# Latent attention scores as row halves plus one stacked rotated product, and bias tables masked one pair per weight piece

## What is computed

```python
def mla_dense(qn, qr, kn, kr, v):
    # qn (B,q,H,64), qr (B,q,H,32), kn (B,k,H,64), kr (B,k,32) shared by the heads, v (B,k,H,64); H = 8
    s = (einsum('bqhd,bkhd->bhqk', qn, kn) + einsum('bqhr,bkr->bhqk', qr, kr)) * (64 + 32) ** -0.5
    p = softmax(s, axis=-1)
    return einsum('bhqk,bkhd->bqhd', p, v)
```

## Time and profile before

| | |
|---|---|
| Runs shown | 2302.57, 2307.16, 2306.70 us; median 2306.7 |
| Profiled execution | 2304.6 us, of which span 2302.8 |
| Granted TensorE clock | 0.996 of full speed |
| PE busy | 2236.8 us, 97% of the span |
| DVE, ACT, POOL busy | 56%, 40%, 12% |
| Chain that ended last | PE 86%, DVE 5%, ACT 3%, ACT's queue 2% |
| DMA queue of ACT | 38914 packets, 33.69 MB |

### The profile page before, as it was taken

How to read it: one execution, slowest core, us unless ns; L and a number is a source line. 1 busy time by engine, 2 the same in 40 slices (tenths; PEclk the granted TensorE clock), 3 DMA queues, 4 the chain that set the end, 5 groups by cost and what they waited for, 6 DMA issues and landing times.

```text
span 2302.8 us, 32992 instructions
## 1 busy us (share of the span) xinstructions
PE 2236.8 (97%) x13479; PEld 1856.5 (81%) x13479; DVE 1294.3 (56%) x1884; ACT 926.4 (40%) x1558; POOL 277.3 (12%) x175
## 2 busy tenths in 40 slices
PE   7999999999999999999999999999989999999999
PEld 7876688888778776688888888888878888888887
DVE  4687558963224778459963225414666562225884
ACT  3447743222214447742222223223655333123773
POOL 2001222121332002221211000000000000000000
PEclk9999999999999999999999999999999999999999
DMA  5220025632983210035532321221000214212221
GB/s 159 87 69 2 1 95 179 198 114 76 235 219 97 83 56 1 7 133 173 165 123 78 128 93 56 78 83 42 15 15 15 81 56 160 84 55 74 68 66 55
DMA packets 149417, 205.80 MB, mean 89 GB/s; under 512 B 42485, under 2 KB 95746, under 8 KB 149250
## 3 DMA queue, kind: packets, MB, share of 16 engines
q1 hardware_dynamic: 110288, 169.83, 22.8%
q10 hardware_dynamic: 38914, 33.69, 5.5%
q0 software_dynamic: 64, 0.16, 0.0%
HBM read 188.85 MB, written 14.82 MB: 88 GB/s over the span
## 4 chain that ended last, share of the span: by engine, by line
PE 86%; DVE 5%; ACT 3%; ACTq 2%; issue 2%; POOL 1%; DMA 1%; POOLq 0%; DVEq 0%
PE ps L526 62%; PE ps L1858 4%; PE ps L1892 3%; PE ps L2509 3%; PE ps L1909 3%; ACTq L2248 2%; PE ps L2526 2%; PE ps L2538 2%; PE ps L2514 1%; PE ps L733 1%; DVE neg_max L2060 1%; DVE probs_t L2116 1%; ACT probs_t L2615 1%; ACT w_high L486 1%; DVE w_low L491 1%
## 5 line engine op out<-in xcount | busy, mean ns | idle before, releaser
L491 DVE TENSOR_TENSOR w_low<-w_raw,w_high 128x2048 fp32r<-128x2048 f32 (+4 forms) x140 | 308.6, 2205 | 497.0 <-ACT w_high L486 496.8
L486 ACT ACTIVATE w_high<-w_raw 128x2048 fp32r<-128x2048 f32 (+4 forms) x140 | 253.0, 1807 | 617.6 <-PE ps L526 559.3
L526 PE MATMUL ps<-h_hi,w_high 128*128 128x512 f32 (+1 forms) x1168 | 439.5, 376 | 1.6 <-DVE h_lo L2906 1.0
L526 PE MATMUL ps<-h_lo,w_high 128*128 128x512 f32 (+1 forms) x1168 | 437.1, 374 | 0.0
L526 PE MATMUL ps<-h_hi,w_low 128*128 128x512 f32 (+1 forms) x1168 | 436.8, 374 | 0.0
L526 PEld LDWEIGHTS ps<-h_hi,w_high 128*128 128x128 f32 x1168 | 220.0, 188 | 42.7 <-issue 1.4
L526 PEld LDWEIGHTS ps<-h_hi,w_low 128*128 128x128 f32 x1168 | 219.8, 188 | 39.7
L526 PEld LDWEIGHTS ps<-h_lo,w_high 128*128 128x128 f32 x1168 | 220.0, 188 | 38.9 <-issue 0.5
L526 PE MATMUL ps<-w_high,h_hi 128*128 128x512 f32 (+3 forms) x576 | 214.0, 372 | 0.7 <-DVE h_lo L2906 0.7
L526 PE MATMUL ps<-w_low,h_hi 128*128 128x512 f32 (+3 forms) x576 | 211.6, 367 | 0.0
L526 PE MATMUL ps<-w_high,h_lo 128*128 128x512 f32 (+3 forms) x576 | 211.3, 367 | 0.0
(11 more groups left out here) (372 smaller groups left out, 3880.5 us busy)
## 6 DMA issues: line engine op xcount, KB each, us to landing
w_raw<-in_w_gate_up SPq DMA_DIRECT2D x44, 1024.0 KB, 5.2
ada_w<-in_ada_w SPq DMA_DIRECT2D x24, 1024.0 KB, 5.2
w_raw<-in_w_down SPq DMA_DIRECT2D x20, 1024.0 KB, 5.1
w_raw<-in_w_in SPq DMA_DIRECT2D x16, 1024.0 KB, 5.1
w_raw<-in_c_in_w SPq DMA_DIRECT2D x16, 1024.0 KB, 5.4
w_raw<-in_w_out SPq DMA_DIRECT2D x8, 1024.0 KB, 5.0
w_raw<-in_ab_in_w SPq DMA_DIRECT2D x8, 1024.0 KB, 5.1
mask_table<-bias_scratch ACTq DMA_DIRECT2D x32, 224.0 KB, 7.8
```

Source lines behind the costliest of these rows:

```text
L486: e.activation(w_high[j % 2][:, 0:size], w_raw[j % 2][:, 0:size], ACT.Copy).then_inc(sig.w_high_done, 1)
L491: e.tensor_tensor(w_low[j % 2][:, 0:size], w_raw[j % 2][:, 0:size], w_high[j % 2][:, 0:size].bitcast(F32), ALU.subtract).then_inc(sig.w_lo ...
L526: mm = e.matmul(dst, lhs, rhs, start=start and a == 0, stop=stop and a == 2)
```

## The change

*Latent scores.* The plain rows of both heads of a pair go into one tile of 128 rows (head 0 in rows 0 to 63, head 1 in rows 64 to 127), and their three products run as row halves in `ORDER`, as in the window. The rotated rows of a head are stacked on 96 rows: the query's as high, high, low and the key's as high, low, high, so that one product on 96 rows gives all three terms. It is added last, except for head 1's context columns, where it comes just before the wait. The stacked keys are the same for all heads and are turned once (two turns at iterations 10 and 11). `rope3` holds three copies of the 32 rotated columns; GpSimd makes those of the next pair's queries after each second unit. The six turns of a pair stand at -4, -4, -3, -3, -2, -2. The queries of window pair 0 are turned before the keys. The queries' evacuation (`QueriesOut`) writes plain and rotated columns apart, two operations for one.

*Bias.* Each piece from 2 to 9 carries the loads of one pair, each from 4 to 11 the store of one.

```diff
-        kvx = at("kvx", [P, NA, BH, 160], F32, R2 + 18432)
+        kvx = at("kvx", [P, NA, 2, BH * 64], F32, R2 + 18432)
+        rope3 = at("rope3", [P, NA, 2, 96], F32, R2 + 18432 + 24576)
...
+        class QueriesOut(InvertedOut):
+            def put(self, e, d, src, mine, m):
+                inv = lat_inv[:, self.group, m:m + 1]
+                for n, (dst, part) in enumerate(zip(d, (src[:, :, 0:64], src[:, :, 64:96]))):
+                    dst = dst.rearrange("p (h w) -> p h w", h=4)
+                    ins = e.activation(dst, part, ACT.Copy, scale=inv) if mine == 0 else e.tensor_scalar(dst, part, inv, None, ALU.mult)
+                ins.then_inc(sig.evac_act if mine == 0 else sig.evac_vec, 1)
...
-                self.paired = [self.local(s) and units[self.steps[s][0]].kind != "mla" for s in range(N)]
+                self.paired = [self.local(s) > 0 for s in range(N)]
...
+                    def rope(dst, m, a, b, block):
+                        return e.matmul(dst.rearrange("p (b c) -> p b c", c=P), x.q_rope(m, block), x.k_rope(a, b), start=False, stop=True)
+
                     if not nl:
                         for c, j in enumerate(js):
                             for n in range(3):
                                 for m in range(2):
-                                    mm = third(self.row(s, m * len(js) + c), m, NT, NA, n, block=x.tiles[j][0])
-                    elif x.kind == "mla":
-                        for m in range(2):
-                            for n in range(3):
-                                third(here[m], m, lo, lo + nl, n)
-                                mm = third(there[m], m, NT, NA, n)
+                                    mm = third(self.row(s, m * len(js) + c), m, NT, NA, n, x.kind != "mla", block=x.tiles[j][0])
+                            for m in range(2 if x.kind == "mla" else 0):
+                                mm = rope(self.row(s, m * len(js) + c), m, NT, NA, x.tiles[j][0])
                     else:
                         for where, n in self.ORDER:
                             m = int(where[1])
+                            if where == "T0" and n == 0 and x.kind == "mla":
+                                rope(there[1], 1, NT, NA, block).then_inc(sig.half_scored, 1)
                             if where == "T0" and n == 0:
                                 e.wait_ge(sig.half_scored, B["half_scored"] + sum(map(bool, self.paired[:s + 1])))
...
+                        if x.kind == "mla":
+                            for m in range(2):
+                                rope(here[m], m, lo, lo + nl, block)
+                            mm = rope(there[0], 0, NT, NA, block)
                     mm.then_inc(sig.scores_ready, 1)
...
+                    if kind in ("parts", "ropes"):
+                        for m in range(2):
+                            ins = e.activation(dst[m], src[:, m * 2 * P:m * 2 * P + 2 * P].rearrange("p (b c) -> p b c", c=P), ACT.Copy)
...
-                    e.tensor_copy(kvx[:, :, :, 128:160], bc(k_rope.unsqueeze(2), [P, NA, BH, 32])).then_inc(sig.rope_staged, 1)
+                    e.tensor_copy(rope3[:, :, 0, :].rearrange("p t (c w) -> p t c w", c=3), bc(k_rope.unsqueeze(2), [P, NA, 3, 32])).then_inc(sig.rope_staged, 1)
...
+                    p = (u - 5) // 2
+                    if not self.grid and u % 2 and 0 <= p < BH // 2:
+                        e.wait_ge(sig.qk_bank, B["qk_bank"] + turned[p] + 1)
+                        for m in range(2):
+                            src = q_b[:, :, 512 + 64 * p + 32 * m:544 + 64 * p + 32 * m]
+                            e.tensor_copy(rope3[:, :, m, :].rearrange("p t (c w) -> p t c w", c=3), bc(src.unsqueeze(2), [P, NA, 3, 32])).then_inc(sig.rope_staged, 1)
...
-            LOADS, STORES = {2: (0, 1), 3: (2, 3), 6: (4, 5), 7: (6, 7)}, {4: (0, 1), 5: (2, 3), 8: (4, 5), 9: (6, 7)}
...
-                for n in self.LOADS.get(j, ()):
+                n = j - 2
+                if 0 <= n < self.PAIRS:
+                    if n >= 2:
+                        e.wait_ge(sig.bias_masked, B["bias_masked"] + n - 1)
                     if n >= 4:
-                        e.wait_ge(sig.bias_stored, B["bias_stored"] + 64)
+                        e.wait_ge(sig.bias_stored, B["bias_stored"] + 16 * (n - 2))
                     for m in range(2):
                         for half in range(2):
...
-                for n in self.STORES.get(j, ()):
+                n = j - 4
+                if 0 <= n < self.PAIRS:
                     e.wait_ge(sig.bias_masked, B["bias_masked"] + n + 1)
                     e.dma_start(masked_dram[n], mask_tables[n % 4][:]).then_inc(sig.bias_stored, 16)
...
-                at_ = [20 + 5 * p + c for c in (-6, -5, -4, -3, -3, -2)]
...
+                at_ = 20 + 5 * p
+                turns.append((at_ - 4, 4 + p, qn[:, 0:4, :], lambda x, f=q_nope: f(x), P, 4, None, ""))
...
+                for m, d in ((0, -4), (1, -3)):
+                    turns.append((at_ + d, 4 + p, stack(m)[:, 0:4, :], lambda x, m=m, f=q_rope: f(x, m), 96, 4, staged, "64"))
...
+                turns.append((at_ - 3, 4 + p, [stack(m)[:, 4:6, :] for m in range(2)], lambda x, f=q_rope: f(4 + x % 2, x // 2), 96, 4, staged, "ropes"))
...
+                turns.append((at_ - 2, 4 + p, kn[:, 0:4, :], lambda x, f=k_nope: f(x), P, 4, None, ""))
...
+                turns.append((at_ - 2, 4 + p, [qn[:, 4:6, :], kn[:, 4:6, :]], lambda x, f=q_nope, g=k_nope: f(4 + x) if x < 2 else g(2 + x), P, 4, None, "parts"))
```

More of the change, by code:

```diff
@@ L1703, in build_program, with __init__ @@
         class WideUnit:
-            def __init__(self, kind, group, head, chunk, t0, tiles, q, k, value, q_low=None, k_low=None):
+            def __init__(self, kind, group, head, chunk, t0, tiles, q, k, value, q_low=None, k_low=None, q_rope=None, k_rope=None):
+                self.q_rope, self.k_rope = q_rope, k_rope
                 self.q_low, self.k_low = q_low, k_low
@@ L1768, in __init__ @@
                 else:
[L1769 removed]
+                    self.counts.update({"keys_staged": 2, "rope_staged": 1 + BH})
             def unit(self, s):
@@ L1875, in scores @@
                             if where[0] == "H":
-                                mm = third(here[m], m, lo, lo + nl, n, mask is None)
+                                mm = third(here[m], m, lo, lo + nl, n, mask is None and x.kind != "mla")
                             else:
-                                mm = third(there[m], m, NT, NA, n)
-                            if where == "T1" and n == 2:
+                                mm = third(there[m], m, NT, NA, n, x.kind != "mla")
+                            if where == "T1" and n == 2 and x.kind != "mla":
                                 mm.then_inc(sig.half_scored, 1)
@@ L2121, in low_turned @@
                     e.wait_ge(sig.qk_high, B["qk_high"] + i + 1)
-                    if kind == "two":
+                    if kind == "parts":
                         src = src.rearrange("p (m b c) -> p m b c", m=2, c=P)
-                        ch.step(e.tensor_tensor(lows[0], src[:, 0], high[:, 0].bitcast(F32), ALU.subtract))
-                        e.tensor_tensor(lows[1], src[:, 1], high[:, 1].bitcast(F32), ALU.subtract).then_inc(sig.qk_ready, 1)
+                        ch.step(e.tensor_tensor(lows[0], src[:, 0], high[0].bitcast(F32), ALU.subtract))
+                        e.tensor_tensor(lows[1], src[:, 1], high[1].bitcast(F32), ALU.subtract).then_inc(sig.qk_ready, 1)
+                    elif kind == "ropes":
+                        src = src[64:96].rearrange("p (m b c) -> p m b c", m=2, c=P)
+                        ch.step(e.tensor_tensor(lows[0], src[:, 0], lows[0].bitcast(F32), ALU.subtract))
+                        e.tensor_tensor(lows[1], src[:, 1], lows[1].bitcast(F32), ALU.subtract).then_inc(sig.qk_ready, 1)
+                    elif kind:
+                        a = int(kind)
+                        e.tensor_tensor(lows, src[a:a + 32].rearrange("p (b c) -> p b c", c=P), lows.bitcast(F32), ALU.subtract).then_inc(sig.qk_ready, 1)
                     else:
@@ L2191, in gpsimd @@
                 if not self.grid:
-                    e.tensor_copy(kvx[:, :, :, 128:160], bc(k_rope.unsqueeze(2), [P, NA, BH, 32])).then_inc(sig.rope_staged, 1)
+                    e.tensor_copy(rope3[:, :, 0, :].rearrange("p t (c w) -> p t c w", c=3), bc(k_rope.unsqueeze(2), [P, NA, 3, 32])).then_inc(sig.rope_staged, 1)
+                turned = [i for i, x in enumerate(self.turns) if x[7] in ("32", "ropes")][1:]
                 for u, x in enumerate(self.units):
@@ L3142, in keys_of @@
                     lows.append(window_k_low[kv][:, a:b, :])
-            keys_of(0)
             for p in range(4):
+                for a, b in ((0, 4), (4, 6)) if p == 3 else ():
+                    turns.append((10 + a // 4, 0, qkv_r[0:96, :, 512:640][:, a:b, :], lambda x, a=a: rope3[:, a + x, 0, :], 96, b - a, ("rope_staged", 1), "32"))
```

(5 more changed lines are left out.)

63 lines of the change are left out of this document (33 added, 30 removed).

## The result

Before: 2303.45 us, median of five runs (2300.69 to 2307.16). After: 2317.9 us (2314.45 to 2319.19), ratio 1.0061 with a 95% interval of 1.0050 to 1.0072. The change makes the kernel slower by 14 us, three times what a measurement can tell from nothing. The forecast was 2312, its range 2300 to 2319.

What follows compares the result with a forecast made beforehand. TensorE, with work for 97% of the span, was taken as the bound. Terms +6.6 + 0.1 + 5.2 + 1.3 - 5.0 - 1.0 + 0.3 = +7.5 us on the profiled 2304.6 gave 2312.1, range 2300 to 2319.

Steps and rivals of the forecast that it cites:

- (b): Latent scores: every switch of array shape costs a full drain, step 2.9 us, kernel 2317; chance 0.12.
- (c): Down projection: the bias stage gives nothing back because ScalarE's issue costs are uneven, kernel 2317; chance 0.10.
- Score steps, +6.6: Sixteen latent score steps grow from 2.20 to 2.61 us, +0.41 each, +6.6 us in all.
- The walk: Piece-by-piece sum of a latent score step from its start, through the wait at head 0's context product: 2.61 us.
- (a): Latent scores: the array overlaps the seam with no drain and a short wait, step 1.98 us, kernel 2302; chance 0.23.
- Context steps, +0.1: Four latent context steps go from 1.51 to 1.54 us, a start and one switch per block: +0.1 us.
- Turns, +5.2 and +1.3: Turns through the spare bank: regrouped latent turns cost +5.2 us over four pairs, two shared-key turns in the window stage +1.3.
- Step five: Last step of a latent pair: its second turn follows the values, so the next pair's scores wait; +2.15 us.
- (d): Latent pairs: the last turn is not late, costing 0.8 us instead of 2.15; kernel 2306 to 2307; chance 0.10.
- Bias, -5.0: Down projection: fewer bias loads between ScalarE's cuts remove both TensorE waits for a low part, -5.0 us.
- Window start, -1.0: Start of window stage: GpSimd's smaller key copy and queries turned ahead of keys save 1.0 us.
- Evacuation and GpSimd's copies, +0.3: Queries' evacuation in two operations and GpSimd's eight new copies, which slow VectorE now and then: together +0.3 us.

Runs made afterwards that it cites:

- the first experiment: The kernel before with only the change's bias part: 2294.99 us, ratio 0.9960 to the kernel before.
- the third experiment: The changed kernel with head 1's rotated context product moved to the front of the latent score step: 2306.93 us, ratio 1.0011 to the kernel before.
- the fourth: The changed kernel with head 1's rotated context product right after head 1's context halves, three half products ahead of the wait: 2313.36 us, ratio 1.0040.

## Why the prediction was right, and where it was not

The sign and the range held, and most mechanisms did. The profiled executions differ by 12.4 us where 7.5 were forecast, and 2317.9 lies outside the 2308 to 2316 that the prediction preferred. That number is the one it gave to the rivals (b) and (c), and neither is what happened: by the time alone the wrong cause would have been named. Point by point:

- **Score steps, +6.6: measured +7.8.** The walk gave 2.61 us, the trace 2.69. Piece by piece it is right but for one: from the step's start to the rotated product at the seam 1.02 us (walk 1.02), from there to the waiting product 0.45 (0.46), to the end of the halves 0.54 (0.54), the three rotated products 0.69 (0.59). The walk priced a change of shape at the 0.085 behind the last product and left out the 0.1 in the first product after it. Rival (a), a step of 1.98, and rival (b), 2.9, are both out. Their two bounds are loosely added: the terms given for (a) come to 2.00, and four drains of 0.16 in place of the one switch of 0.085 would make 3.2.
- **Context steps, +0.1: measured +1.4** (1.88 us against 1.51), of which 1.1 lie before the last one's scores. Mis-sized for the same reason: the walk charged a start of 0.1 and a switch of 0.085 per block, and the step has one start and three changes of 0.2.
- **Turns, +5.2 and +1.3: measured 4.5 + 0.6 and 0.9**, 6.0 in all where 6.5 were forecast. Step five rose by 2.39 us (forecast 2.15), the first two steps fell to 3.14 (3.15), step three rose to 4.31 (4.14), and step four, forecast unchanged at 4.14, to 4.43. The +1.3 does not follow from its own terms, 0.72 + 1.24 - 0.43, which give 1.5. Rival (d), a last turn that isn't late, is out: the wait is there four times.
- **TensorE's clock: no term, measured +6.9.** This is the step that failed. "So 1718.5 instead of 1716.34, +2.15" prices a wait of TensorE at its length. The wait of 1.5 to 1.8 us was forecast, its consequence not: behind three waits of four the clock fell to half. Fillers in the same wait, or no wait, remove it.
- **Bias, -5.0: measured -7.6.** 1.6 of the difference is the same omission with the other sign: the wait of 2.8 us in the earlier trace rows had a stretch at a granted clock of 0.60 behind it, and the profile before showed it to whoever asked for the windows there. The other 1.0 is what the waits cost beyond their listed length. Rival (c) is out, as the first experiment shows by itself.
- **Window start, -1.0: measured -0.8,** though half the reason given, the queries' turn ahead of the keys, does nothing by itself.
- **Evacuation and GpSimd's copies, +0.3: measured 0.** From the end of the down projection to the window stage the two executions take the same time to within 0.1 us.
- The remaining 1.2 us lie ahead of everything that the change touches: the slow stretch at 269 us that only the execution before had.

What the clock adds in one place (+6.9) it takes back in others (-1.6 and, by the luck of two executions, -1.2); the sum came nearer than its parts.

It stays open what decides which wait loses the clock. It isn't the pair: the change lost it at the first, third and fourth, the third experiment at the first and third, the fourth at the second and fourth, with the same waits in all of them. There is one trace of each kernel, so how often each place loses it is not known either.

## What to carry to other kernels

When a wait of TensorE is priced, the granted clock in the windows behind it has to be read as well. In this kernel three of four waits listed at 1.5 to 1.8 us cost another 1.3 to 2.9, one listed at 2.8 cost 4.7, and the fourth and one of 2.1 had no slow stretch behind them; a few idle products in the waits were free. Small products of different array shapes are worth sorting by shape, since each change, in either direction, costs 0.2 us, nearly what a product of 512 columns streams (0.235). Two profiled executions of the same code can differ by a slow stretch of their own, so a difference of 1 or 2 us is read only after the granted clock of both. And a change with two parts is best timed as two: here a part worth 8.5 us was buried under one that costs 23.

## What the runs showed of the hardware

- The granted clock fell to 0.50, with 0.64 and 0.65 on either side, after TensorE, otherwise full, had stood for 0.8 and then 1.5 us (windows after, 1672 to 1688). With the same pattern of work it fell at three pair starts of four in the change, and at two, not the same ones, in each of the third and fourth experiments.
- A change between the full array and row halves costs 0.2 us in either direction: 0.09 behind the last product of a group, 0.10 in the first of the next (1707.88 to 1709.21 in the change). One change less in a context step took 0.22 us off it.
- Four DMA issues on ScalarE's queue took between 4.5 and 9.5 us for loads of the same size: what a queue is charged per issue is uneven by a factor of two.
- VectorE's two copies of 768 columns beside one GpSimd copy: the first, begun 0.02 us before GpSimd's, took 0.56 us, and the second ended 0.41 us after GpSimd's, whether that took 1.86 us (before) or 1.06 (after).
